# In the first turn of the experts, the second run of gathers moves behind the last gate tile, and the gate products wait for their own chunk only

## The chip, the cores and the metric

The kernel runs on one core of a Trainium2 chip. The metric is the device time of one execution in microseconds (us); the runs shown are three executions of the same program. Five engines work side by side and meet at semaphores: TensorE (PE, with its weight loads shown apart as PEld), VectorE (DVE), ScalarE (ACT), GpSimd (POOL) and SyncE (SP), which here issues the loads of the weights.

## The reference, cut to what matters

Two blocks are computed on 256 tokens of width 1024. The second one has two layers, and each ends in a mixture of 32 experts of width 256, of which every token uses two:

```
act = jax.nn.silu(jnp.einsum("td,edh->teh", t, w_g[sl])) * jnp.einsum("td,edh->teh", t, w_u[sl])
out = out + jnp.einsum("teh,ehd->td", act * combine[:, sl, None], w_d[sl])
```

`t` are the modulated tokens, `combine` holds the router's weights (zero but for the two chosen experts), and `sl` picks the experts of one group. This mixture, run once in each of two layers, is the only place that the change touches.

## The kernel before

The experts are taken in pairs: `PAIRS` is 16, and a **turn** `p` works on pair `p`. An expert has 64 places (`SLOTS`) for its tokens, so a pair fills 128. Token rows are picked by products with 0/1 matrices (`select`), which is called a gather; the tokens lie in a high and a low part (`hhi`, `hlo`), and both are multiplied. One gather serves four experts (two turns) for one chunk `c` of 128 of the 1024 features, and is four matmuls into PSUM. ACT or DVE then scales, shifts and writes it to `xg`. The weights come in tiles of 512 KB, twelve for each pair: eight (`gu`, k = 0 to 7, one for each chunk of features, gate and up side by side) and four (`d`). SP loads them in their order of use into a ring of 16 places (`RING`), and loads a place again when the semaphore `pe_tile` says that PE has used the tile that lay there.

`moe_events` writes the order of the work once, and PE, ACT and DVE each walk it, doing only their part of an event. The events are:

- `first` c: the gather of chunk c for turns 0 and 1, into PSUM bank c % 4. Even chunks are written to `xg` by ACT (semaphore `g_high`), odd ones by DVE (`g_copy`).
- `rest` j: DVE writes more columns of `select` (`slots_ready`).
- `gu` p, k: two products of `xg` with weight tile k for each of the two experts, into bank 0. The first of a turn waits for `mprod`, since it writes over bank 0.
- `V` p: PE turns `select` round into bank 1, ACT copies it (`selectT_ready`), DVE sums two numbers from it (`wslot_read`).
- `G` p, k: two gathers for a later pair of turns into bank 1, the first and second run of a turn (k = 0, 1). ACT writes both to `xg` (`g_high`). The second run waits until the first has been read.
- `A` p: ACT takes silu of the gate half of bank 0, and DVE multiplies it with the up half (`mprod`).
- `T` p: PE transposes that product; `d`: the down products; `Y` and `S`: scale the result and scatter it to the tokens.

On PE, `gu` (0, 0) waits in `gather_read` for all eight chunks of `first`, and the other seven products of turn 0 then wait for their weight tile alone. The events of turn 0, which has no `T`, `d`, `Y` or `S`, run: `gu` 0, `gu` 1, `gu` 2, `gu` 3, `V`, `gu` 4, `G` 0, `gu` 5, `gu` 6, `G` 1, `gu` 7, `A`. Turn 1 begins with `gu` 0, `gu` 1, `T` 0. The semaphore waits that matter are these:

```python
# gather_read
eng.wait_ge(s("g_high"), G_ACT_ALL * l + DC // 2 + 2 * p)
eng.wait_ge(s("g_copy"), G_DVE_ALL * (l + 1))
# ACT, event A
act.wait_ge(s("pe_tile"), moe_tile(l, "gu", p, 7) + 1)
act.activation(pair_a[:, 0, :], work[0][:, 0:T], ACT.Silu).then_inc(s("msilu"), 1)
```

In the rows below L1415 is a matmul of a gather, L1461 one of `gu`, L1435 one of `V`, L1474 one of `T`, L1486 one of `d`. On ACT, L1914 writes `xg`, L1922 is `V`, L1931 is the silu of `A`. On DVE, L2661 is `rest`, L2717 writes `xg`, L2728 is `V`, L2732 is the product of `A`.

Of the kernel before, what the change touches and what calls it, by code (L numbers as in the profile page):

```python
# [113 lines left out]
def moe_events(event):  # L114


    def turn(p):
        d, scatter, gather = p >= 1, p >= 2, p // 2 + 1 < FOURS
        event("gu", p, 0)
        if p == 0:  # L120
            event("rest", 0, 1)
        event("gu", p, 1)
        if d:
            event("T", p - 1, 0)
        event("gu", p, 2)
        if p == 0:
            event("rest", 0, 2)
        event("gu", p, 3)
        event("V", p, 0)
        if scatter:  # L130
            for j in range(3):
                event("S", p - 2, j)
        event("gu", p, 4)
        if d:
            event("d", p - 1, 0)
            event("d", p - 1, 1)
        if gather:
            event("G", p, 0)
        event("gu", p, 5)
        event("gu", p, 6)  # L140
        if d:
            event("d", p - 1, 2)
        if gather:
            event("G", p, 1)
        event("gu", p, 7)
        event("A", p, 0)
        if d:
            event("d", p - 1, 3)
            event("Y", p - 1, 0)
            event("Y", p - 1, 1)  # L150
    for c in range(DC):
        event("first", 0, c)
    event("rest", 0, 0)
    for p in range(PAIRS):
        turn(p)
    event("T", PAIRS - 1, 0)
    event("d", PAIRS - 1, 0)
    event("d", PAIRS - 1, 1)
    event("S", PAIRS - 2, 0)
    event("S", PAIRS - 2, 1)  # L160
    event("Y", PAIRS - 1, 0)
    event("S", PAIRS - 2, 2)
    event("d", PAIRS - 1, 2)
    event("d", PAIRS - 1, 3)
    event("Y", PAIRS - 1, 1)
    for j in range(3):
        event("S", PAIRS - 1, j)
# [3 lines left out]
G_ACT_ALL, G_DVE_ALL = DC // 2 + 2 * (PAIRS - 2), DC // 2  # L171
# [83 lines left out]
def moe_tile(l, what, p, k):  # L255
    return START[f"moe{l}"] + moe_place(what, p, k)
# [200 lines left out]
def program(nc, wstream, ada_d, c_d, consts_d, params_d, x_d, mem_d, rows_d, out_d):  # L457
    with ExitStack() as ctx:
        sems = {}

        def s(name):
            name = SHARED.get(name, (name, 0))[0]
            if name not in sems:
                sems[name] = ctx.enter_context(nc.semaphore(name))
            return sems[name]
# [146 lines left out]
        def gather_read(eng, l, p):  # L612

            eng.wait_ge(s("g_high"), G_ACT_ALL * l + DC // 2 + 2 * p)
            eng.wait_ge(s("g_copy"), G_DVE_ALL * (l + 1))
# [132 lines left out]
        def _(pe):  # L748
# [63 lines left out]
            def tile_ready(r, i=None, turn=6):  # L812
                if r in NUMBER:
                    pe.wait_ge(s("lo_done"), along(NUMBER[r] + 1, i, turn))
                    return whi[NUMBER[r] % AHEAD], wlo[NUMBER[r] % AHEAD]
                tile_loaded(pe, r, i, turn)
                return tiles[SLOT[r]], None
# [303 lines left out]
            def event(what, n, part=None):  # L1121
# [169 lines left out]
                elif what == "cmp_values":  # L1291
                    pe.wait_ge(s("pct_ready"), 1)
                    for j in range(HPG):
                        for g in range(GROUPS):
                            mm = pe.matmul(work[2 + j // 2][DH * g:DH * g + DH, (j % 2) * T:(j % 2) * T + T],
                                           vcmp[:, g, j, :], pcT[:, g, :],
                                           start=False, stop=False, skip_group_check=True)
                    mm.then_inc(s("cmp_values"), 1)
            mixer_events(event)

            pe.wait_ge(s("olo_ready"), 6)
# [14 lines left out]
            for l in range(LAYERS):  # L1316
                k = 7 + 3 * l
# [94 lines left out]
                def gather(bank, c, sel, at=0):  # L1412
                    for j, tok in enumerate((tok_hi, tok_lo)):
                        for q in range(QT):
                            mm = pe.matmul(work[bank][:, at:at + T], tok[:, q * D + c * P:q * D + (c + 1) * P],  # L1415
                                           sel(q), start=(j + q == 0), stop=(j + q == 2), skip_group_check=True)
                    return mm

                def event(what, p, k):
# [21 lines left out]
                    elif what == "G":  # L1441
                        if k == 0:
                            pe.wait_ge(s("selectT_ready"), base + p + 1)
                            pe.wait_ge(s("wslot_read"), 2 * (base + p + 1))
                        else:
                            pe.wait_ge(s("g_high"), G_ACT_ALL * l + DC // 2 + 2 * p + 1)
                        n = 2 * (p // 2 + 1)
                        for j in range(2):
                            mm = gather(1, 4 * (p % 2) + 2 * k + j,
                                        lambda q: select[:, q, n:n + 2, :].rearrange("p n t -> p (n t)"), j * T)  # L1450
                        mm.then_inc(s("g_mm"), 1)
                    elif what == "gu":
                        if k == 0 and p % 2 == 0:
                            gather_read(pe, l, p)
                        if k == 0:
                            pe.wait_ge(s("mprod"), base + p)
                        r = moe_tile(l, "gu", p, k)
                        w, _ = tile_ready(r)
                        for e in range(2):
                            a = (2 * (p % 2) + e) * SLOTS  # L1460
                            mm = pe.matmul(work[0][SLOTS * e:SLOTS * e + SLOTS, :], xg[:, p // 2 % 2, k, a:a + SLOTS],  # L1461
                                           w[:, e * 512:(e + 1) * 512], start=(k == 0), stop=(k == DC - 1),
                                           skip_group_check=True)
                        mm.then_inc(s("pe_tile"), 1)
                    elif what == "T":
                        pe.wait_ge(s("mprod"), base + p + 1)
                        pe.wait_ge(s("act_turned"), base + p)
                        if p < PAIRS - 2:
                            pe.wait_ge(s("g_high"), G_ACT_ALL * l + DC // 2 + 2 * (p + 1))
                        else:  # L1470
                            pe.wait_ge(s("selectT_ready"), base + p + 1)
                            pe.wait_ge(s("wslot_read"), 2 * (base + p + 1))
                        for f in range(2):
                            mm = pe.transpose(work[1][:, T + f * P:T + (f + 1) * P], pair_b[:, 0, f * P:(f + 1) * P], ident)  # L1474
                        mm.then_inc(s("turn_mm"), 1)
                    elif what == "d":
                        if k == 0:
                            pe.wait_ge(s("act_turned"), base + p + 1)
                        if p >= 1 and k % 2 == 0:
                            pe.wait_ge(s("y_low"), 2 * (base + p) - 1 + k // 2)  # L1480
                        r = moe_tile(l, "d", p, k)
                        w, _ = tile_ready(r)
                        half, f = k // 2, k % 2
                        for e in range(2):
                            own = slice(SLOTS * e, SLOTS * e + SLOTS)
                            mm = pe.matmul(work[2 + half][own, :], turned[:, f, own], w[:, e * 512:(e + 1) * 512],  # L1486
                                           start=(f == 0), stop=(f == 1), skip_group_check=True)
                        mm.then_inc(s("pe_tile"), 1)
                    elif what == "S":
                        if k == 0:  # L1490
                            pe.wait_ge(s("y_low"), 2 * (base + p) + (1 if p == PAIRS - 1 else 2))
                        sel = selectT[:, p, :]
                        for m in range(*S_PART[k]):
                            if p == PAIRS - 1 and m == DC // 2:
                                pe.wait_ge(s("y_low"), 2 * (base + p) + 2)
                            for y in (yshi, yslo):
                                mm = pe.matmul(acc_c[:, m, :], y[:, m * P:(m + 1) * P], sel, start=False,  # L1497
                                               stop=False, skip_group_check=True)
                            if (p, m) in S_LAST:
                                mm.then_inc(s("s_last"), 1)  # L1500
                        if k == 2:
                            mm.then_inc(s("s_mm"), 1)
                moe_events(event)
            norm_sum(7 + 3 * LAYERS)
            norm_row(7 + 3 * LAYERS, 0)
# [1423 lines left out]
```

## Time and profile before

| | |
|---|---|
| median of 3 runs | 1733.84 us (1732.2 to 1735.55) |
| the profiled execution's own time | 1735.7 us |
| its span in the trace | 1734.0 us |
| PE busy | 1660.4 us, 96% of the span |
| DVE, ACT busy | 936.6 us (54%), 647.7 us (37%) |
| chain that ended last | PE 75%, DVE 15%, ACT 7% |

An execution's own time is 1.7 us above its span. A busy share is the time in which an engine had an instruction at work; the chain is followed back from the last instruction, at each step to what released it. The two runs of the experts lie at 1011 to 1280 us and at 1451 to 1720 us from the span's start.

### The profile page before, as it was taken

Reading aid. Unit: us, or ns where it says so; the run is one execution under the profiler, and the core shown is the slowest. Engines: PE = TensorE matmul, PEld = TensorE weight load, DVE = VectorE, ACT = ScalarE, POOL = GpSimd, SP = SyncE. Lnnn points to the kernel's source line nnn. Section 1 sums busy time; section 2 is a strip of 40 time slices with the busy share of each in tenths; the row PEclk is TensorE's granted clock in tenths of the full one; section 3 lists DMA queues with packets and bytes.
Section 4 is the critical chain, followed back from the end, with each engine's and each line's share of the span. In section 5 each row is a group of like instructions: output and inputs, shape, how many; then the busy total and the mean of one; then the engine's idle time right before and its main releaser. Section 6 shows DMA issues by size and latency. Waiting matters only on the chain.

```text
span 1734.0 us, 29081 instructions
## 1 busy us (share of the span) xinstructions
PE 1660.4 (96%) x11261; PEld 1331.7 (77%) x11271; DVE 936.6 (54%) x1654; ACT 647.7 (37%) x1060; POOL 3.7 (0%) x9
## 2 busy tenths in 40 slices
PE   9999999999989999999999989999999998999998
PEld 8999989899878989999898954444469895444444
DVE  6888878753454768888697641111149864111112
ACT  5543456223355543333513332222243243222222
POOL 0000000000000000000000000000000000000000
PEclk9999999898799999999899999999999999999998
DMA  8998835113333549888243659999944355999993
GB/s 309 364 364 306 282 133 182 60 39 103 129 109 123 169 155 349 306 304 289 102 147 112 250 201 389 376 391 378 385 174 146 113 203 220 379 388 380 382 386 133
DMA packets 115806, 420.96 MB, mean 243 GB/s; under 512 B 12944, under 2 KB 13088, under 8 KB 115568
## 3 DMA queue, kind: packets, MB, share of 16 engines
q1 hardware_dynamic: 114624, 414.19, 65.3%
q0 software_dynamic: 1072, 5.21, 0.8%
q8 instruction: 80, 1.31, 0.3%
q14 instruction: 30, 0.25, 0.1%
HBM read 416.73 MB, written 2.62 MB: 242 GB/s over the span
## 4 chain that ended last, share of the span: by engine, by line
PE 75%; DVE 15%; ACT 7%; issue 3%; DVEq 0%; ACTq 0%
PE work L825 19%; PE work L1461 12%; PE acc L825 11%; DVE yconv L2496 6%; PE work L1486 5%; PE work L917 5%; PE work L1415 4%; PE acc L1497 3%; PE work L785 2%; ACT whi L1521 2%; ACT xg L1914 2%; PE work L860 2%; DVE wlo L1968 2%; PE work L902 1%; PE work L795 1%
## 5 line engine op out<-in xcount | busy, mean ns | idle before, releaser
L1968 DVE TENSOR_TENSOR wlo<-raw,whi 128x1024 fp32r<-128x1024 f32 x264 | 321.5, 1224 | 190.7 <-ACT whi L1521 190.2
L1521 ACT ACTIVATE whi<-raw 128x1024 fp32r<-128x1024 f32 x264 | 277.1, 1056 | 284.7 <-PE work L825 188.0
L825 PE MATMUL work<-hhi,whi 128*128 128x256 f32 x1024 | 293.2, 286 | 1.7 <-DVE hlo L1996 0.8
L825 PE MATMUL work<-hlo,whi 128*128 128x256 f32 x1024 | 291.6, 285 | 0.0
L825 PE MATMUL work<-hhi,wlo 128*128 128x256 f32 x1024 | 291.4, 285 | 0.0
L825 PEld LDWEIGHTS work<-hhi,whi 128*128 128x128 f32 x1024 | 198.2, 194 | 3.8 <-DVE wlo L1968 2.5
L825 PEld LDWEIGHTS work<-hlo,whi 128*128 128x128 f32 x1024 | 198.3, 194 | 0.1
L825 PEld LDWEIGHTS work<-hhi,wlo 128*128 128x128 f32 x1024 | 198.3, 194 | 0.0
L2732 DVE TENSOR_TENSOR pair_b<-work,pair_a 128x256 f32<-128x256 f32 x32 | 13.6, 425 | 309.5 <-ACT pair_a L1931 309.5
L1914 ACT ACTIVATE xg<-work,mod,gscale 128x256 f32<-128x256 f32 x120 | 61.7, 561 | 224.6 <-PE work L1415 224.6
L1461 PE MATMUL work<-over_splits,xg 128*64 128x512 f32 x480 | 120.8, 607 | 6.7 <-DVE pair_b L2732 6.2
L2074 DVE SCALAR_TENSOR_TENSOR ada_tiles<-ada_tiles,c_act 128x1024 f32<-128x1024 f32 x96 | 116.3, 1219 | 1.7 <-DMA ada_tiles<-ada_d 1.7
L860 PE MATMUL work<-hf,raw 128*128 128x256 f32 x512 | 113.3, 383 | 0.0
L860 PEld LDWEIGHTS work<-hf,raw 128*128 128x128 f32 x512 | 98.8, 193 | 13.9
L1461 PE MATMUL work<-raw,xg 128*64 128x512 f32 x408 | 101.7, 606 | 4.3 <-DVE pair_b L2732 2.3
L825 PE MATMUL acc<-ahi,whi 128*128 128x256 f32 x352 | 99.5, 283 | 2.9 <-DVE alo L2109 2.9
L917 PE MATMUL work<-hhi,whi 128*128 128x256 f32 x288 | 86.8, 302 | 15.2 <-ACT gates L1529 10.7
L2496 DVE SCALAR_TENSOR_TENSOR yconv<-vpad,params,yconv 128x256 f32<-128x256 f32 x240 | 99.4, 479 | 1.4
L825 PE MATMUL acc<-alo,whi 128*128 128x256 f32 x352 | 98.9, 281 | 0.0
L825 PE MATMUL acc<-ahi,wlo 128*128 128x256 f32 x352 | 98.7, 281 | 0.0
L917 PE MATMUL work<-hlo,whi 128*128 128x256 f32 x288 | 84.9, 295 | 0.0
L917 PE MATMUL work<-hhi,wlo 128*128 128x256 f32 x288 | 83.8, 291 | 0.0
(426 smaller groups left out, 2985.9 us busy)
## 6 DMA issues: line engine op xcount, KB each, us to landing
raw<-wstream_d SPq DMA_DIRECT2D x448, 512.0 KB, 4.7
over_splits<-wstream_d SPq DMA_DIRECT2D x192, 512.0 KB, 5.9
ada_tiles<-ada_d SPq DMA_DIRECT2D x96, 512.0 KB, 5.2
over_pool<-wstream_d SPq DMA_DIRECT2D x48, 512.0 KB, 6.2
bias_rows_d<-rt POOLq DMA_DIRECT2D x1, 1536.0 KB, 11.4
xT<-x_d SPq DMA_DIRECT2D x4, 256.0 KB, 4.2
mem_in<-mem_d POOLq DMA_DIRECT2D x1, 1024.0 KB, 5.3
tb<-bias_rows_d POOLq DMA_DIRECT2D x1, 1024.0 KB, 7.3
```

The lines of the kernel that those rows point to most:

```text
L825: mm = pe.matmul(out, a, b, start=(start and k == 0), stop=(stop and k == n - 1), skip_group_check=skip)
L860: mm = pe.matmul(work[bank][:, 0:T], h[:, c * P:(c + 1) * P], hf[:, c, :], start=(c == 0), stop=(c == DC - 1))
L917: mm = pe.matmul(bank[:, 0:T], ((h, h, l)[k % 3])[:, c * P:(c + 1) * P], ((hhi, hlo, hhi)[k % 3])[:, c, :], start=(k == 0), stop=(k == 23))
L1415: mm = pe.matmul(work[bank][:, at:at + T], tok[:, q * D + c * P:q * D + (c + 1) * P], sel(q), start=(j + q == 0), stop=(j + q == 2), skip_ ...
L1461: mm = pe.matmul(work[0][SLOTS * e:SLOTS * e + SLOTS, :], xg[:, p // 2 % 2, k, a:a + SLOTS], w[:, e * 512:(e + 1) * 512], start=(k == 0), ...
L1486: mm = pe.matmul(work[2 + half][own, :], turned[:, f, own], w[:, e * 512:(e + 1) * 512], start=(f == 0), stop=(f == 1), skip_group_check=True)
L1497: mm = pe.matmul(acc_c[:, m, :], y[:, m * P:(m + 1) * P], sel, start=False, stop=False, skip_group_check=True)
L1521: act.activation(whi[n % AHEAD][:], tiles[SLOT[SPLITS[n]]][:], ACT.Copy).then_inc(s("hi_done"), 1)
L1914: return act.activation(out, src, ACT.Identity, bias=mod[:, b:b + 1], scale=gscale[:, g:g + 1])
L1968: dve.tensor_tensor(wlo[n % AHEAD][:], tiles[SLOT[SPLITS[n]]][:], whi[n % AHEAD][:].bitcast(F32), ALU.subtract).then_inc(s("lo_done"), 1)
L2074: dve.scalar_tensor_tensor(ada_tiles[:, k, :], ada_tiles[:, k, :], 1.0, c_act[:], ALU.mult, ALU.mult, accum_out=out).then_inc(s("ada_done" ...
L2496: ins = dve.scalar_tensor_tensor(yconv[:, c, :], vpad[:, c, i:i + T], w, yconv[:, c, :], ALU.mult, ALU.add)
```

## The change

Three things, all for turn 0 of the experts alone, in both layers. The event `G` 0, 1 stands behind `gu` 7 and `A`, and no longer between `gu` 6 and `gu` 7. The first gate product on PE waits for the first three chunks that ACT writes (chunks 0, 2 and 4; bank 0, into which it writes, held chunks 0 and 4). Each later gate product of turn 0 waits for its own chunk, on `g_high` or `g_copy`, beside its weight tile.

```diff
@@ moe_events, turn(p)
         event("gu", p, 6)
         if d:
             event("d", p - 1, 2)
-        if gather:
+        if gather and p > 0:
             event("G", p, 1)
         event("gu", p, 7)
         event("A", p, 0)
+        if gather and p == 0:
+            event("G", p, 1)
         if d:
             event("d", p - 1, 3)
             event("Y", p - 1, 0)
@@ PE, event gu
                     elif what == "gu":
-                        if k == 0 and p % 2 == 0:
+                        if p == 0 and k % 2 == 0:
+                            pe.wait_ge(s("g_high"), G_ACT_ALL * l + max(k // 2 + 1, 3))
+                        elif p == 0:
+                            pe.wait_ge(s("g_copy"), G_DVE_ALL * l + k // 2 + 1)
+                        elif k == 0 and p % 2 == 0:
                             gather_read(pe, l, p)
                         if k == 0:
                             pe.wait_ge(s("mprod"), base + p)
```

On PE, the first products of turn 0 behind the gathers of `first` (`work<-select` is a gather, `work<-raw,xg` a gate product; the names in brackets are the semaphores waited for, `loaded` with a number being the weight tile's place). Before:

```order
L1415 MATMUL work<-select,hlo 128x256 x2
L1461 MATMUL work<-raw,xg 64x512 [waits mprod,loaded5,g_copy,g_high]
L1461 MATMUL work<-raw,xg 64x512
L1461 MATMUL work<-raw,xg 64x512 [waits loaded0]
L1461 MATMUL work<-raw,xg 64x512
L1461 MATMUL work<-raw,xg 64x512 [waits loaded1]
```

After:

```order
L1417 MATMUL work<-select,hlo 128x256 x2
L1467 MATMUL work<-raw,xg 64x512 [waits loaded5,mprod,g_high]
L1467 MATMUL work<-raw,xg 64x512
L1467 MATMUL work<-raw,xg 64x512 [waits loaded0,g_copy]
L1467 MATMUL work<-raw,xg 64x512
L1467 MATMUL work<-raw,xg 64x512 [waits loaded1,g_high]
```

The instructions are the same; the first product has lost its wait for `g_copy` and asks a lower count of `g_high`, and each later tile has gained one wait.

On PE, the end of turn 0 and the first product of turn 1 (`over_pool` and `over_splits` are weight tiles as `raw` is). Before:

```order
L1461 MATMUL work<-over_pool,xg 64x512 [waits loaded6]
L1461 MATMUL work<-over_pool,xg 64x512
L1415 MATMUL work<-select,hhi 128x256 [waits g_high]
L1415 MATMUL work<-select,hhi 128x256
L1415 MATMUL work<-select,hlo 128x256 x2
L1415 MATMUL work<-select,hhi 128x256 x2
L1415 MATMUL work<-select,hlo 128x256 x2
L1461 MATMUL work<-over_pool,xg 64x512 [waits loaded7]
L1461 MATMUL work<-over_pool,xg 64x512
L1461 MATMUL work<-over_splits,xg 64x512 [waits loaded11,mprod]
```

After:

```order
L1467 MATMUL work<-over_pool,xg 64x512 [waits loaded6,g_high]
L1467 MATMUL work<-over_pool,xg 64x512
L1467 MATMUL work<-over_pool,xg 64x512 [waits loaded7,g_copy]
L1467 MATMUL work<-over_pool,xg 64x512
L1417 MATMUL work<-select,hhi 128x256 [waits g_high]
L1417 MATMUL work<-select,hhi 128x256
L1417 MATMUL work<-select,hlo 128x256 x2
L1417 MATMUL work<-select,hhi 128x256 x2
L1417 MATMUL work<-select,hlo 128x256 x2
L1467 MATMUL work<-over_splits,xg 64x512 [waits loaded11,mprod]
```

The second run of gathers now lies between the last gate product of turn 0 and the product of turn 1 that waits for `mprod`.

On ACT, the same place, from the first run's write of `xg` to the copy of `T` 0 (L1934, L1940 after). Before:

```order
L1914 ACTIVATE xg<-work,mod,gscale 128x256 [waits g_mm]
L1914 ACTIVATE xg<-work,mod,gscale 128x256
L1914 ACTIVATE xg<-work,mod,gscale 128x256 [waits g_mm]
L1914 ACTIVATE xg<-work,mod,gscale 128x256
L1931 ACT_TABLE_LOAD
L1931 ACTIVATE pair_a<-work 128x256 [waits pe_tile]
L1934 ACTIVATE pair_a<-work 128x256 [waits turn_mm]
```

After:

```order
L1920 ACTIVATE xg<-work,mod,gscale 128x256 [waits g_mm]
L1920 ACTIVATE xg<-work,mod,gscale 128x256
L1937 ACT_TABLE_LOAD
L1937 ACTIVATE pair_a<-work 128x256 [waits pe_tile]
L1920 ACTIVATE xg<-work,mod,gscale 128x256 [waits g_mm]
L1920 ACTIVATE xg<-work,mod,gscale 128x256
L1940 ACTIVATE pair_a<-work 128x256 [waits turn_mm]
```

The load of silu's table and the silu have moved ahead of the write of the second run, and no further table load has come in. DVE and SP have the instructions that they had, in the same order.

## Rows read from the trace of the kernel before

**Rows 1.** The page, busy time of each engine over the span.
```profile
PE 1660.4 (96%) x11261; PEld 1331.7 (77%) x11271; DVE 936.6 (54%) x1654; ACT 647.7 (37%) x1060; POOL 3.7 (0%) x9
```

**Rows 2.** Windows in the experts: us, each engine's busy time, PEclk, DMA share, GB/s.
```profile
1017.00:1037.00 20.00, 17.58 (x86) 7.14 (x86) 5.26 (x12) 4.86 (x9) 0.00 (x0) 1.00 0.79 283
...
1217.00:1237.00 20.00, 19.92 (x108) 9.30 (x106) 2.15 (x5) 5.22 (x11) 0.00 (x0) 1.00 1.00 383
```

**Rows 3.** Timeline, layer 0, turn 0 begins: start us, us, engine, line, work [idle].
```profile
1014.42 0.40 PE L1415 MATMUL work<-select,hhi 128*128 128x256 f32 x2
...
1015.09 0.56 ACT L1914 ACTIVATE xg<-work,mod,gscale 128x256 f32<-128x256 f32 x1 [0.53 <-PE work L1415]
...
1015.57 0.54 DVE L2717 TENSOR_SCALAR xg<-work,gscale,mod 128x256 f32<-128x256 f32 x1 [0.40 <-PE work L1415]
...
1016.07 0.40 PE L1415 MATMUL work<-select,hlo 128*128 128x256 f32 x2
1016.51 0.54 DVE L2717 TENSOR_SCALAR xg<-work,gscale,mod 128x256 f32<-128x256 f32 x1 [0.40 <-PE work L1415]
...
1017.16 3.65 PE L1461 MATMUL work<-raw,xg 128*64 128x512 f32 x16 [0.68 <-ACT xg L1914]
```

**Rows 4.** Timeline, layer 0, the end of turn 0.
```profile
1023.59 1.02 ACT L1914 ACTIVATE xg<-work,mod,gscale 128x256 f32<-128x256 f32 x2 [1.82 <-PE work L1415]
...
1024.39 1.03 PE L1461 MATMUL work<-over_pool,xg 128*64 128x512 f32 x4
...
1025.35 0.50 PE L1415 MATMUL work<-select,hhi 128*128 128x256 f32 x2
...
1026.16 0.40 PE L1415 MATMUL work<-select,hlo 128*128 128x256 f32 x2
...
1026.48 1.08 PE L1461 MATMUL work<-over_pool,xg 128*64 128x512 f32 x4
1026.59 1.02 ACT L1914 ACTIVATE xg<-work,mod,gscale 128x256 f32<-128x256 f32 x2 [1.98 <-PE work L1415]
1027.63 1.28 ACT L1931 ACT_TABLE_LOAD   x1
1028.92 0.38 ACT L1931 ACTIVATE pair_a<-work 128x256 f32<-128x256 f32 x1
1029.34 0.42 DVE L2732 TENSOR_TENSOR pair_b<-work,pair_a 128x256 f32<-128x256 f32 x1 [7.12 <-ACT pair_a L1931]
...
1029.82 1.94 PE L1461 MATMUL work<-over_splits,xg 128*64 128x512 f32 x8 [2.26 <-DVE pair_b L2732]
```

**Rows 5.** Timeline of PE, layer 1, the same two places.
```profile
1457.15 3.65 PE L1461 MATMUL work<-raw,xg 128*64 128x512 f32 x16 [0.68 <-ACT xg L1914]
...
1469.81 1.94 PE L1461 MATMUL work<-over_splits,xg 128*64 128x512 f32 x8 [2.26 <-DVE pair_b L2732]
```

**Rows 6.** Timeline, layer 0, `rest` and `V` of turn 0, and the first run.
```profile
1016.97 4.23 DVE L2661 TENSOR_TENSOR select<-consts,rt 128x256 fp32r<-128x256 f32 x6
...
1020.74 0.44 PE L1435 MATMUL work<-identr,select 128*128 128x128 f32 x2
...
1021.38 0.39 ACT L1922 ACTIVATE selectT<-work 128x256 fp32r<-128x256 f32 x1 [4.79 <-PE work L1438]
1021.87 0.35 DVE L2728 TENSOR_REDUCE rt<-work 64x1 f32<-64x2 f32 x2 [0.67 <-ACT selectT L1922]
...
1022.36 0.48 PE L1415 MATMUL work<-select,hhi 128*128 128x256 f32 x2
```

**Rows 7.** Timeline of ACT, layer 0, its table load ahead of the first gather's write.
```profile
1010.66 1.28 ACT L1914 ACT_TABLE_LOAD   x1 [4.88 <-DVE overflow L2658]
...
1012.29 0.56 ACT L1914 ACTIVATE xg<-work,mod,gscale 128x256 f32<-128x256 f32 x1 [0.34 <-PE work L1415]
```

**Rows 8.** Waits of SP's DMA queue, 1000 to 1270 us: total us, times, longest.
```profile
SPq L654 <- PE work L1461: 141.2, 118, 20.6
```

**Rows 9.** DMA issues of 1200 to 1240 us: count, KB each, median us to landing.
```profile
over_splits<-wstream_d SPq DMA_DIRECT2D x16, 512.0 KB, 6.6
```

## The prediction

> **What bounds the kernel now.** I read the busy shares first: PE is at work 96% of the span [rows 1]. A change can then win where PE stands still, or by taking work from it, and this one takes no work. So I looked at the windows through the experts. In the steady part PE is busy 19.92 of 20 us, but in the first window of a layer's experts only 17.58 [rows 2]: some 2.4 us are idle there, and that is the stretch that the diff edits. The timeline of that stretch shows where they are. The reader is to look for the brackets on PE's rows. Of idle time above 0.1 us that a wait explains there are two pieces, 0.68 us ahead of the first gate product of turn 0 [rows 3] and 2.26 us ahead of the first gate product of turn 1 [rows 4]. In layer 1 the same two rows carry the same 0.68 and 2.26 [rows 5]. Every later engine in the experts works from what PE gives it, and PE's own stream hardly pauses after this, so what is won here should reach the end.
>
> **The first wait: chunks instead of all of them.** Before, the first gate product waits for the last copy, which is DVE's of chunk 7: it starts at 1016.51 and takes 0.54, so it ends at 1017.05, and the product starts at 1017.16 [rows 3]. (The row names ACT as the releaser; ACT's write of chunk 6 was done before, DVE's end fits the start.) After, it needs the third write of ACT, 1015.09 + 0.56 = 1015.65 [rows 3]. That is earlier than PE itself is ready. PE's last pair of gather matmuls starts at 1016.07 [rows 3], and the distance from such a last pair to a gate product with nothing to wait for is 1026.48 - 1026.16 = 0.32 us [rows 4]. The product would start at 1016.39, **0.77 us earlier**. The later ones have slack: chunk 5 is there at 1015.57 + 0.54 = 1016.11, chunk 7 at 1017.05 [rows 3], and five gate products, at about 0.86 us each, run before chunk 5 is asked for.
>
> The added waits, one for each of seven tiles, I cost at nothing. The nearest rows are the gathers of chunks 4 to 7, each of which waits for `g_high` or `g_copy` too: the pairs of matmuls from 1014.42 to 1016.07 are seven steps, 0.236 us a step, without a break at the chunk's border [rows 3]. The bound from the other side is the 0.68 us that PE stood still when such a wait was really late; it is priced below, as a rival.
>
> **What limits the shift at once.** `V` moves from 1020.74 to 1019.97, ACT's copy from 1021.38 to 1020.61 (0.39 long, done at 1021.00), and DVE's two sums could start at 1021.87 - 0.77 = 1021.10. But DVE is then in the six selections of `rest`, which hang on its copy of chunk 7 and don't move: 1016.97 + 4.23 = 1021.20 [rows 6]. The sums start 0.10 later than the shift would have them. The first run of gathers waits for them (it starts 0.49 behind their start), so it moves from 1022.36 to 1021.69: **0.67 us are left of the 0.77**. `V` itself needs the first two selections and chunk 7's copy; both are there long before 1019.97.
>
> **The second wait: the last gate tile ahead of the gathers.** Before, the order on PE is `gu` 6 at 1024.39, the second run at 1025.35, `gu` 7 at 1026.48, and then nothing until 1029.82 [rows 4]. In between lies a chain on two other engines: ACT writes the second run (1026.59, 1.02 us), loads silu's table (1.28), takes silu (0.38), DVE multiplies (0.42), and PE goes on. With the shift of 0.67, after the change:
>
> - `gu` 6 starts at 1023.72. A gate tile is four matmul records. Sixteen in a row take 3.65 us [rows 3] and four 1.08, so each further record adds 0.214, and `gu` 7 starts 0.86 later, 1024.58.
> - The second run follows a gate tile by 1025.35 - 1024.39 = 0.96, so at 1025.54, and what stands behind it follows by 1026.48 - 1025.35 = 1.13: the first gate product of turn 1 could start at **1026.67**, as far as PE goes.
> - ACT is free of the first run at 1023.59 + 1.02 - 0.67 = 1023.94. Its table load then ends by about 1025.24. `gu` 7 ends at 1024.58 + 1.03 = 1025.61, and silu can start at about 1025.64. From silu's start to PE's next gate product it is 1029.82 - 1028.92 = 0.90 [rows 4]: 1026.54.
>
> The later of the two is PE's own, by 0.13 us. The product of turn 1 moves from 1029.82 to 1026.67, **3.15 us earlier**, first gain included. What covers the ACT chain is the second run of gathers, 1.13 us of PE work that was on the path before and is on it still; were it shorter by over 0.13, the rest would be idle.
>
> That the table load is out of the way needs that ACT takes it before it waits for `gu` 7. In the order it stands ahead of the silu, and the wait is written on the silu. The earlier load shows that this holds: ACT begins it at 1010.66, and the activation behind it, which waits for the gather, at 1012.29, idle for 0.34 us after the load [rows 7].
>
> The Trainium skill (ScalarE: Activation LUTs, What ACT_TABLE_LOAD costs) states 1.28 us for the load and 1.38 us more for a drain, 2.66 us for each switch. This trace has the 1.28 but shows no drain: the write of `xg` ends at 1027.61 and silu starts at 1028.92. By the page's figure silu would start at 1026.60 after the change and turn 1 at 1027.50, an estimate from that page, and both layers together would give 4.6 us; I go by the row.
>
> **Who waits next.** ACT's write of the second run now stands behind silu. Its last pair starts at 1025.54 + 0.81 and ends 0.40 later, 1026.75; ACT is done with silu at 1026.02. The write ends near 1027.80. `T` 0 needs it and comes two gate products after 1026.67, near 1028.5: hidden by 0.7 us. SP gets the weight tiles' places earlier, below. Nothing else is moved past anything.
>
> **The sum.** 3.15 us in layer 0, and layer 1 has the same idle pieces [rows 5], so 6.3 us. Against the profiled execution's own 1735.7 us that is 1729.4; that execution lies 1.9 us above the median, so against the median, 1733.84 - 6.3 = **1727.5 us**, 0.36% faster. Nothing under 0.2% (3.5 us) can be told from no change here.
>
> **The rivals.**
>
> *The weights don't come faster.* The DMA engines' share in the steady part is 1.00, at 383 GB/s [rows 2]. If the stream of weights were what really paces the experts, PE would start each layer 3 us earlier and wait for tiles later, and the time would stay at **1733.8**. For it speaks that full share. Against it: over 1000 to 1270 us the queue of loads waited 141.2 us for PE to free a place, in 118 waits [rows 8]. At 383 GB/s a tile of 524,288 bytes takes 1.37 us, a turn of the ring of 16 places 21.9 us, and 6.6 us after its issue a tile is there [rows 9]. So it lies ready some 15 us before its use, five times what is won. Chance 0.10.
>
> The Trainium skill (HBM Reference, Specifications) puts a core's part of the memory's bandwidth at about 358 GB/s, and says that a core streaming alone gets more, about 425. The trace, at 383, is above the first figure; only the first would make this rival the likeliest.
>
> *The table load stays on the path*, because ACT takes it only when `gu` 7 is done. Silu then starts at 1025.64 + 1.30 = 1026.94, turn 1 at 1027.84; 1.98 us a layer, 4.0 in all: **1729.8**. Rows 4 alone allow it, since there the load begins just as both conditions are met; rows 7 speak against it. Chance 0.09.
>
> *The single waits cost more than the idle time they replace.* Each of turn 0's seven later tiles has two waits now. If PE could no longer bring the next tile's stationary operand in ahead of such a wait, each border would cost up to the 0.68 us of a late one. Seven are 4.8 us a layer against 3.15 won: 1.6 lost, twice, **1737.1**. It decides from 0.45 us a border. Against it stand the gathers of chunks 4 to 7, with their waits and no break [rows 3]. Chance 0.04.
>
> **How the numbers follow.** The forecast, 5 to 7 us won, gets 0.73; the rivals 0.10, 0.09 and 0.04; 0.04 is left for what I don't see. The range must cover the forecast, the table's rival at 1729.8 and the scatter of the median (some 1.7 us either way in the runs of before): 1725.0 to 1731.6. It leaves out the weights' rival and the slower one. Faster by over 0.2%, that is below 1730.4: nearly all of the forecast and some two thirds of the table's rival, 0.80. Within 0.2%: the weights' rival, a third of the table's and a little of the rest, 0.15. Slower: 0.05.
>
> **What the changed profile would show.** First product of turn 0 about 0.32 us after the last gather pair and no bracket of 0.68 on it; DVE's sums right at the end of the selections; ACT's table load starting at the end of the first run's write, over before `gu` 7 ends; the first product of turn 1 with no idle time above some 0.1 us, 10.3 us after the first of turn 0 where it was 12.7; the first window with PE busy above 19; and SP's waits for PE still there through the experts, with tiles landing in 5 to 7 us. It is wrong if PE shows waits for DMA later in the experts, if the table load begins only behind `gu` 7, or if turn 0's tiles stand further apart than 0.86 us.

## The result

Four runs of the changed kernel have a median of 1722.69 us (1721.74 to 1724.3), against 1733.16 us of before; the ratio is 0.9932, 95% interval 0.9916 to 0.9948. It is 10.5 us faster, where 6.3 were forecast; the time lies 2.3 us below the range. Timed again (run 2 below) the ratio is 0.9942 (0.9928 to 0.9956), 10.0 us. So both the forecast's mechanism and something that it left out have to be found in the traces. Two disturbed executions of run 17 (1850.79 and 8536.54 us) stand in no mean below.

### The edited stretch, after

Timeline of the changed kernel in layer 0, the rows that answer to [rows 3, 4 and 6] (start us, us, engine, line, work, idle before it):

```profile
1012.87 0.39 PE L1417 MATMUL work<-select,hlo 128*128 128x256 f32 x2
1013.19 3.65 PE L1467 MATMUL work<-raw,xg 128*64 128x512 f32 x16
...
1013.76 4.22 DVE L2667 TENSOR_TENSOR select<-consts,rt 128x256 fp32r<-128x256 f32 x6
...
1017.91 0.34 DVE L2734 TENSOR_REDUCE rt<-work 64x1 f32<-64x2 f32 x2
...
1019.62 1.02 ACT L1920 ACTIVATE xg<-work,mod,gscale 128x256 f32<-128x256 f32 x2 [1.82 <-PE work L1417]
1020.42 1.89 PE L1467 MATMUL work<-over_pool,xg 128*64 128x512 f32 x8
1020.66 1.28 ACT L1937 ACT_TABLE_LOAD   x1
...
1022.24 0.51 PE L1417 MATMUL work<-select,hhi 128*128 128x256 f32 x2
1022.36 0.39 ACT L1937 ACTIVATE pair_a<-work 128x256 f32<-128x256 f32 x1 [0.41 <-PE work L1467]
...
1022.77 0.42 DVE L2738 TENSOR_TENSOR pair_b<-work,pair_a 128x256 f32<-128x256 f32 x1 [4.52 <-ACT pair_a L1937]
...
1023.38 1.94 PE L1467 MATMUL work<-over_splits,xg 128*64 128x512 f32 x8
1023.49 1.02 ACT L1920 ACTIVATE xg<-work,mod,gscale 128x256 f32<-128x256 f32 x2 [0.75 <-PE work L1417]
```

Both brackets of idle time are gone from PE. The first gate product stands 0.32 us behind the last pair of gathers (1.09 before), and the first product of turn 1 comes 10.19 us behind that of turn 0 (12.66 before; 10.28 forecast). Together 0.77 + 2.47 = 3.24 us a layer. The table load runs while PE is still in the last two gate tiles, ACT then waits 0.41 us for the last of them, and its write of the second run follows silu without holding anybody. In layer 1 PE's two first products stand at 1449.92 and 1460.10, 10.18 apart.

The windows that answer to [rows 2] (us, each engine's busy time, PEclk, DMA share, GB/s) show PE at work all through the first 20 us. The transfers' share rose in the first window, 0.86 for 0.79, and is 0.99 for 1.00 in the steady part:

```profile
1013.00:1033.00 20.00, 20.00 (x103) 8.59 (x103) 5.66 (x12) 6.27 (x12) 0.00 (x0) 1.00 0.86 319
1213.00:1233.00 20.00, 19.91 (x106) 9.14 (x105) 2.15 (x5) 5.38 (x11) 0.00 (x0) 1.00 0.99 377
```

SP's waits for gate products over 1000 to 1270 us are 138.7 us in 116 waits, where [rows 8] had 141.2 in 118. PE's own waits over 1018 to 1275 us are 2.1 us for the product of silu, 0.5 for ACT and 0.4 for DVE, and none for a weight tile.

### The rest of the difference

The spans are 1734.0 and 1722.0 us, 12.0 apart, and the edits account for 2 x 3.24 = 6.5. The remainder lies where the two programs are the same, at the start and at the end. The first weight products, and the 32 small matmuls of the last norm's sum, before:

```profile
16.23 0.55 PE L825 MATMUL work<-hhi,whi 128*128 128x256 f32 x1 [0.82 <-DVE hlo L1996]
16.58 0.42 PE L825 MATMUL work<-hlo,whi 128*128 128x256 f32 x1
...
1719.73 6.04 PE L785 MATMUL work<-ones,hf 128*128 128x1 f32 x32 [0.33 <-ACT hf L1534]
```

The same in the changed kernel:

```profile
14.56 0.35 PE L827 MATMUL work<-hhi,whi 128*128 128x256 f32 x1 [0.82 <-DVE hlo L2002]
14.75 0.28 PE L827 MATMUL work<-hlo,whi 128*128 128x256 f32 x1
...
1710.00 3.70 PE L787 MATMUL work<-ones,hf 128*128 128x1 f32 x32 [0.33 <-ACT hf L1540]
```

The reader is to compare the duration of like matmuls: 0.42 against 0.28 us, and 6.04 against 3.70 for the same 32 at the end. That is the clock's lower and upper level (1.2 and 2.4 GHz). The windows say so for the end, where the granted clock is 0.56 over 1720 to 1726 us before and 1.00 over 1710 to 1714 after. For the start the durations alone speak, since the window of 15 to 20 us has 1.00 in both; but in run 16 the same products took 0.55 and 0.44 us, and the granted clock of that window is 0.50 there. The changed kernel is 3.2 us ahead when it comes to the first gather of layer 0 (1007.82 against 1011.03), and wins 2.3 us more in the last sum. Whether that is chance or comes with the edit is what most of the experiments are about.

### The profile page after: what moved, and what is told of

Read it like the earlier page. It is cut to its first block, busy times and chain, and to the rows that moved or that the text cites. A ratio compares the mean times of both kernels' runs of the same rounds, so it can differ in the third digit from the quotient of the medians.

```text
span 1722.0 us, 29103 instructions
## 1 busy us (share of the span) xinstructions
PE 1653.5 (96%) x11271; PEld 1323.7 (77%) x11271; DVE 935.8 (54%) x1654; ACT 647.5 (38%) x1060; POOL 3.7 (0%) x9
## 4 chain that ended last, share of the span: by engine, by line
PE 75%; DVE 15%; ACT 6%; issue 3%; DMA 0%; SPq 0%; DVEq 0%; ACTq 0%
PE work L827 19%; PE work L1467 13%; PE acc L827 11%; DVE yconv L2502 6%; PE work L1492 5%; PE work L919 5%; PE work L1417 4%; PE acc L1503 3%; PE work L787 2%; ACT whi L1527 2%; DVE wlo L1974 2%; PE work L862 2%; ACT xg L1920 2%; PE work L904 1%; PE work L797 1%
```

## The experiments

"Mean" is that of all timed runs; the profile is of one of them. Ratios are to the kernel before on the same chip. "Theory A" and its fellows are the readings that the expectations set against each other.

**Run 1, before again.** No edit.

> The kernel of before, unchanged, timed against itself. In the profiles the edited stretches gave 3.4 us in layer 0 and 3.4 us in layer 1, which is 6.7 of the 12.0 us between the two spans; 3.2 us more came in the first 65 us of the program and 2.2 us in its last 10 us, where TensorE's granted clock stood at its lower level in the one and at its upper level in the other. Theory A, the two further pieces come from where the clock happens to stand in an execution: this copy scatters by 2 to 4 us from run to run, a ratio of 1.000 with an interval of 0.15% or more, and its profile may show another clock at the start or the end than before's. Theory B, they belong to the program: the copy repeats before's start (first products at 16.2 us, half clock) and end (32 products of the last sum in 6.0 us).

Ratio 1.000 (0.9989 to 1.001), mean 1735.15 of 12. The trace repeats before's start (16.13 us) and even each mark up to 1719 us within 0.4 us, but its last sum took 3.70 us, not 6.04. So the start belongs to the program as profiled (for theory B), and the end doesn't (for theory A).

**Run 2, the changed kernel again.** No edit.

> The changed kernel as it is, timed again beside before on one chip. Theory A (the clock at the start and the end is chance): on average over ten runs a gain nearer to 6.5 us than to 10.5, with single runs from 1722 to 1731. Theory B (a property of the program): again 10.5 us, 1722 to 1724, and again a full clock at 14.6 us and in the last sum (3.7 us).

Ratio 0.9942, mean 1725.62 of 6, 1723.84 to 1726.75: 10 us again, tightly. The trace has the upper clock at the start (first weight product at 14.62) and in the last sum (3.70). "Nearer to 6.5" is refuted.

**Run 3, the waits alone**

```diff
-                        if k == 0 and p % 2 == 0:
+                        if p == 0 and k % 2 == 0:
+                            pe.wait_ge(s("g_high"), G_ACT_ALL * l + max(k // 2 + 1, 3))
+                        elif p == 0:
+                            pe.wait_ge(s("g_copy"), G_DVE_ALL * l + k // 2 + 1)
+                        elif k == 0 and p % 2 == 0:
```

> Only the waits of the gate products of turn 0 are changed; the second run of gathers stays ahead of the last gate tile. Between the first gather and the first product of turn 1 it should win 0.67 us in each layer (0.77 less what the selections on DVE hold back), 1.3 us in all: that step of the prediction. Theory A: total 1.3 us give or take 2. Theory B: if the further 4 to 5 us hang on the program being changed at all, 5 to 6 us.

Ratio 0.9985 (0.9973 to 0.9997), mean 1734.09. In layer 0 it is 18.06 us from the first gather to turn 1, where before has 18.79: 0.73, a little above the expected 0.67. In layer 1 it is 19.35 us against 18.91, because the gathers ran at the lower clock (granted 0.50 over 1447 to 1453 us); from turn 0's first product to turn 1's it is 12.66 as in every trace of the old order. The trace shows a second thing there, in the product behind the idle 2.26 us:

```profile
1027.80 1.94 PE L1465 MATMUL work<-over_splits,xg 128*64 128x512 f32 x8 [2.26 <-DVE pair_b L2736]
...
1466.55 3.33 PE L1465 MATMUL work<-over_splits,xg 128*64 128x512 f32 x8 [2.26 <-DVE pair_b L2736]
```

The same eight matmuls behind the same idle time took 1.94 us in layer 0 and 3.33 in layer 1. Over 1466 to 1472 us the granted clock is 0.72. PE stood still for 2.26 us and its clock fell. From turn 1's start to DVE's first write of `xT` behind the experts it then took 249.84 us, where layer 0 of the same trace took 248.25: the fall cost 1.6 us.

**Run 4, the move alone**

```diff
-        if gather:
+        if gather and p > 0:
             event("G", p, 1)
         event("gu", p, 7)
         event("A", p, 0)
+        if gather and p == 0:
+            event("G", p, 1)
```

> Only the second run of gathers is moved behind the last gate tile; the first product still waits for all eight chunks. Between the first gather and the first product of turn 1 it should win 2.4 to 2.5 us in each layer, 4.9 us in all. Rival of the prediction (silu's table load stays on the path): 1.2 us a layer. Theory A: total 4.9 us give or take 2. Theory B: 9 us.

Ratio 0.9964 (0.9953 to 0.9976), mean 1729.93, 6 us. The stretch takes 16.57 and 16.44 us: 2.2 and 2.5 won. The table load's rival is out, the first wait of 0.68 us is there as before. The parts, 2 and 6 us, make some 8, not 10; but each is known to 2 us only, so this doesn't yet show that more than the sum is there. Behind the experts of layer 0 this trace lost 1.9 us to before's, though it has no idle time ahead of turn 1: more on this below.

**Run 5, before with a longer start and a held end.** `hold` issues matmuls on zeros.

```diff
-            hold(1, 8)
-            norm_sum(0)
+            hold(1, 24)
+            norm_sum(0, (0, 2, 2, 2))
...
-            norm_row(0, 0)
+            norm_row(0, 12)
...
-            norm_sum(7 + 3 * LAYERS)
+            norm_sum(7 + 3 * LAYERS, (2, 2, 2, 2))
```

> The kernel before with more matmuls on zeros that nobody reads: 24 for 8 at the start, two ahead of each part of the first norm's sum, 12 behind its row, and two ahead of each part of the last norm's sum. They are to bring TensorE's clock up before the first weight products and hold it up in the last sum. Theory A, the further 3 to 4 us of the changed kernel come from the clock at the start: this one starts its weight products at the upper level (pairs 0.12 us apart, not 0.21) and reaches the first gather of layer 0 some 3 us nearer to the changed kernel's time; in all 2 to 4 us faster than before, unless the 16 more matmuls delay the first sum by up to 2 us. Theory B, the further gain has its cause in the experts: no change against before, or slower by the added matmuls.

Ratio 0.9993 (0.9984 to 1.0002), mean 1734.02. The weight products started at 21.43 us for 16.23, and the first gather came at 1010.73 for 1011.03: what the clock gave, the longer start took, and the expected 2 to 4 us did not come.

**Run 6, the changed kernel with the same.**

> The changed kernel with the same added matmuls on zeros. Theory A: with the same clock at start and end in both, the difference to the kernel before with these matmuls is that of the edited stretches, 6.3 to 6.8 us, and not 10. Theory B: it stays 10 us.

Ratio 0.9946 (0.9927 to 0.9965), mean 1726.07. The pair's means differ by 8.0 us, between the two expectations; the two traces differ by 6.9, with the first gather at 1010.73 and 1010.34.

**Run 7, silu behind the second run on ScalarE**, TensorE as changed.

```diff
-        event("A", p, 0)
         if gather and p == 0:
             event("G", p, 1)
+        event("A", p, 0)
```

> The changed kernel, but ScalarE (and with it VectorE) takes silu of turn 0 behind its write of the second run of gathers, as before the change; TensorE's program is that of the changed kernel, instruction for instruction. The write ends at 1024.51 in the changed kernel's trace, the table load takes 1.28 and from silu's start to the next product it is 0.90: turn 1 should start near 1026.7 instead of 1023.4, 3.3 us lost a layer, 6.6 in all, about 1732. If the cover by the second run of gathers were not what matters, it would lose less than 2. Theory A (start and end by chance of the clock) or a start that goes with TensorE's program: its first products start at the upper clock as the changed kernel's do (14.6 us) if the start goes with TensorE's program, at either level if it is chance.

Ratio 1.0001 (0.9985 to 1.0016), mean 1735.10: the whole gain is gone. PE's rows:

```profile
1027.93 2.37 PE L1467 MATMUL work<-over_splits,xg 128*64 128x512 f32 x8 [3.27 <-DVE pair_b L2738]
...
1030.85 2.84 PE L1467 MATMUL work<-over_splits,xg 128*64 128x512 f32 x8
```

The idle time is 3.27 us, as worked out (3.3), and what stands behind it ran at the lower clock (2.84 for the usual 1.94; granted 0.77 over 1026 to 1032 us). In layer 1 the same 3.27 us left the clock up. Against the changed kernel's trace 6.66 us are lost in the two edited stretches, 1.7 by this fall and 1.85 in the code behind the experts of layer 0. PE's program is that of the changed kernel, but the first weight product took 0.55 us (at 14.30), the lower level: the start doesn't go with PE's program.

**Run 8, the new order in every turn**

```diff
-        if gather and p > 0:
-            event("G", p, 1)
         event("gu", p, 7)
         event("A", p, 0)
-        if gather and p == 0:
+        if gather:
             event("G", p, 1)
```

> The changed kernel, with the second run of gathers behind the last gate tile and silu in every turn that gathers, not in turn 0 alone. In the changed kernel's trace TensorE still waits 2.1 us a layer for the product of silu, in 7 turns, 0.3 us each, since ScalarE writes the second run (1.02 us) ahead of silu. With silu first that wait should go: 2 us a layer, 4 us in all, against the changed kernel. Rival: the transposes of the next turn wait for the later write of the run; they come two gate products behind, 1.9 us, and the write ends 1.4 us after the run, so nothing is lost there.

Ratio 0.9897 (0.9875 to 0.9918), median 1718.55, mean 1718.07: the fastest kernel of the study, 7.5 us below the changed kernel's mean. The waits for the product of silu have left the list; this is all that 1015 to 1265 us has:

```profile
PE work L1490 <- ACT pair_a L1938: 0.5, 1, 0.5
```

From turn 1's first product to DVE's first write of `xT` it took 245.1 us in layer 0 and 245.0 in layer 1, the changed kernel 248.3 and 248.2: 3.2 us a layer, where 2 were expected. Only 2.1 us of it are the waits that the list had; where the rest comes from stays open. Its start was at the lower clock (16.21 us) as before's was.

**Run 9, the idle time filled**, in the kernel before.

```diff
+                        if (p, k) == (1, 0):
+                            for _ in range(7):
+                                pe.matmul(work[2][:, :], zero[:, :], spread(zero[:, 0:1], (512,), (0,)),
+                                          start=True, stop=True)
```

> The kernel before, with seven matmuls on zeros (0.21 us each, 1.5 in all) into a bank that is free then, between the last gate product of turn 0 and the first of turn 1, where TensorE stands idle for 2.26 us. The path is untouched: profiled span and edited stretches as before (12.66 us from turn 0's first product to turn 1's). Theory C: in a part of the executions the clock falls behind that idle time, as in the waits-only kernel's layer 1, where the eight products behind it took 3.33 us and not 1.94; closing the idle time saves that too. Then this kernel's mean lies 1 to 2 us under before's and its slow runs (1738 to 1741) are rarer. Without theory C: mean the same within 0.5 us.

Ratio 0.9998 (0.999 to 1.0007), mean 1734.63 against 1734.84 of the 23 executions of before beside it. The path is untouched (12.66 us), the idle time 0.63. None of its 11 executions was above 1735.7; of before's 23 executions six were, from 1736.3 to 1741.6. Four of these six have a mean granted clock of 0.960, and none of the 11 is below 0.962. That fits theory C without showing it, and the mean moved by 0.2 us, not 1 to 2.

**Runs 10, 11, 13 to 16, other starts.** `hold(1, 8)` becomes `hold(1, 12)`, `(1, 10)` and `(1, 16)`, in the kernel before and in the changed one.

> The kernel before with 12 matmuls on zeros at the start for 8, so that TensorE is at work for longer before the first norm's sum. Theory A: its clock rises within these, the 32 products of the first sum take some 3.7 us and not 7.0, its weight products start at the upper level, and it is 2 to 3 us faster than before. Rival: the four more only delay the sum by 1 to 2 us and the clock rises no sooner.

> The changed kernel with the same 12 matmuls at the start. Its start was at the upper clock for the first sum already, so it should gain nothing or lose up to 1 us. Theory A: against the kernel before with 12, 6.4 us from the edited stretches and what theory C adds, 7 to 8 us, not 10.

> The kernel before with 10 matmuls on zeros at the start for 8: only the place of the clock's changes against the program is shifted. Theory A: mean within 2 us of before's, edited stretches 37.7 us as in every trace of this order. Theory D: the same; the pair decides.

> The changed kernel with 10 for 8. Edited stretches 31.3 to 31.5 us. Theory A: the difference of this pair's means differs from the 10 us by 2 or more and is between 5 and 9. Theory D: 9 to 10 us again.

> The kernel before with 16 for 8: the start shifts further. Same reading as with 10; 0 to 3 us slower for the longer wait of the first sum.

> The changed kernel with 16 for 8. Theory A: a third value for the pair's difference, with the mean over all pairs near 7. Theory D: 9 to 10 us once more.

The ratios of before's order are 0.9999, 1.0006 and 0.9994 (12, 10, 16), those of the changed order 0.9947, 0.9939 and 0.9941. The start alone is worth nothing that can be told, though with 12 and 16 the first gather came 1.8 and 2.0 us earlier than in the trace of before, and the gain is 9 to 12 us in each pair: theory A, as far as it means the start, isn't borne out. (In runs 10 and 11 the first weight product took 0.55 us, so the rise of the clock by then, which run 10 was to bring, didn't come.) The traces show other differences. In the pair with 16 the first gather comes at 1009.05 and 1008.97 us, so the start is level, and still the spans differ by 8.9: 6.4 in the edited stretches and 2.3 behind turn 1 of layer 1, which is the last sum. And in two of the three traces of before's order the clock fell behind the 2.26 us. Run 10:

```profile
1028.35 2.66 PE L1461 MATMUL work<-over_splits,xg 128*64 128x512 f32 x8 [2.26 <-DVE pair_b L2732]
```

Run 13:

```profile
1027.56 2.52 PE L1461 MATMUL work<-over_splits,xg 128*64 128x512 f32 x8 [2.26 <-DVE pair_b L2732]
```

**Run 12, all turns with 12 at the start and the end held**

> A version that may beat all: the second run of gathers and silu in the new order in every turn, 12 matmuls on zeros at the start, and two ahead of each part of the last norm's sum. All turns alone gave 1718.1 us on average with a start at the lower clock; the start should add 2 us, the end 1 us where the clock falls in the last sum: 1715 to 1716. Rival: the start brings nothing, 1717 to 1718.

Ratio 0.9916 (0.9904 to 0.9929), mean 1719.40. 1715 to 1716 were expected. Its profiled execution is the fastest of those profiled (1716.53), but the mean isn't under run 8's: the added matmuls bring nothing that can be told.

**Runs 17 and 18, level.** Both with 16 at the start and the last sum held as in run 5; the kernel before also with run 9's filling.

> The kernel before with 16 matmuls on zeros at the start, seven in the idle time ahead of turn 1, and two ahead of each part of the last norm's sum: the clock is held up in both places where traces of the old order lose it. Theory E (the surplus is the clock at these two places): 1.9 us from the end and 1 us from the idle time, 1731 to 1732 on average, against 1734.1 with the 16 alone. If they are not the cause: 1734.

> The changed kernel with the same 16 at the start and the same matmuls in the last sum (it has no idle time ahead of turn 1 to fill). Theory E: the end costs it 0.5 us, 1725.1, and the difference to the levelled kernel before is the 6.4 us of the edited stretches, 6 to 7. Otherwise the difference stays at 9 to 10.

The means are 1732.9 of ten and 1726.0 of six, 6.9 us apart. By the ratios, 0.9990 (0.9977 to 1.0003) and 0.9944 (0.9925 to 0.9962), it is 8 us. Run 17 was expected at 1731 to 1732: it missed that, and its ratio can't be told from 1. The two traces are only 3.8 us apart, because the start now goes the other way (first gather at 1007.63 and 1010.48). So this pair fits theory E without proving it.

## Why the prediction was wrong

What each trace says, from the starts on PE's timeline and the span ("between" is from turn 1 of layer 0 to the first gather of layer 1, "rest" from turn 1 of layer 1 to the end):

| trace | first gather | gather to turn 1, layers 0, 1 | between | rest |
|---|---|---|---|---|
| before | 1011.03 | 18.79, 18.91 | 421.08 | 264.2 |
| run 1, before again | 1011.02 | 18.82, 18.92 | 421.21 | 261.9 |
| run 9, filled | 1010.57 | 18.83, 18.91 | 421.13 | 264.1 |
| run 10, before, 12 | 1009.20 | 19.15, 18.90 | 424.37 | 261.8 |
| run 13, before, 10 | 1008.53 | 19.03, 18.93 | 424.39 | 264.2 |
| run 15, before, 16 | 1009.05 | 18.90, 18.92 | 421.24 | 264.2 |
| run 3, waits alone | 1009.74 | 18.06, 19.35 | 419.40 | 265.4 |
| run 4, move alone | 1010.30 | 16.57, 16.44 | 423.15 | 261.8 |
| run 7, silu behind | 1009.03 | 18.90, 19.01 | 424.54 | 261.8 |
| changed | 1007.82 | 15.56, 15.69 | 421.03 | 261.9 |
| run 2, changed again | 1007.89 | 15.82, 15.65 | 420.98 | 261.9 |
| run 11, changed, 12 | 1007.15 | 15.74, 15.67 | 420.97 | 261.9 |
| run 14, changed, 10 | 1007.98 | 15.58, 15.67 | 421.10 | 261.9 |
| run 16, changed, 16 | 1008.97 | 15.69, 15.69 | 421.18 | 261.9 |

**The mechanism was right, in both halves.** 3.0 to 3.5 us a layer in the pairs of traces without a held end, 3.25 on average, where 3.15 were worked out. The first wait gave 0.77. The 0.10 us that the selections on DVE were to hold back were not there: DVE's sums started 4.72 us behind the first gate product, as before (4.71), and overlapped the end of the selections by 0.07. That is why turn 1 came at 10.19 and not 10.28. Silu's chain was covered by the second run of gathers as drawn; run 7 took that cover away and lost it all. The added waits cost nothing (turn 0's first 16 gate products took 3.65 us as before), and the three rivals are out: no table load on the path, no wait for weights. One reading was loose, without effect on the sum: the 2.4 us that [rows 2] have idle are nearly all the 2.26, since the 0.68 lie ahead of that window but for their last 0.16.

**The step that failed is the sum**, "against the median, 1733.84 - 6.3": it took for granted that all code outside the edited stretches keeps its time, and let only the scatter of a median widen the range, which it took from the 3.4 us between three executions. Later executions of before lie between 1730.3 and 1741.6 us. The code outside has a clock that changes with when it runs. In the two traces compared first it gave 3.2 us at the start and 2.3 in the last sum, 5.5 of the 12.0. Over all traces four places show:

- *The last norm's sum.* Its 32 matmuls took 5.6 to 6.1 us in five of the seven traces with before's order on PE and an unheld end (before, runs 3, 9, 13 and 15) and 3.70 in the other two (1 and 10). In all five of the changed kernel they took 3.70, and in runs 4, 7 and 8 too. 2.3 us hang on it.
- *The clock behind the idle 2.26 us.* It fell in 3 of the 14 places that the traces of kernels with this idle time offer (runs 3, 10 and 13), once in two behind run 7's 3.27 us, and never at this place in the traces without such idle time. From turn 1 to DVE's first write of `xT` a layer took 248.2 to 248.3 us without a fall, whatever the order of turn 0 (runs 8 and 12 apart, which change the later turns), and 249.8 to 250.0 with one: a fall cost 1.6 to 1.8 us. With that frequency it is some 0.7 us an execution, over both layers, as an estimate. The prediction priced this idle time at its own length; the trace that it read from happened to be one in which the clock held.
- *The start.* The first gather comes 3.1, 2.1, 0.6, 0.1, 0.4 and -2.9 us earlier in the changed member of the six pairs (runs 1 and 2, 10 and 11, 13 and 14, 15 and 16, 5 and 6, 17 and 18); over the kernels with different starts the timed mean moved by nothing that can be told.
- *The norm's sum behind the experts of layer 0.* "Between" is 424.4 in runs 10 and 13 for 421.2, and only half of the 3.2 us more is the fall. The other half is in this sum, the same kind of matmuls with one column, here in before and in run 10:

```profile
1281.36 4.72 PE L785 MATMUL work<-ones,hf 128*128 128x1 f32 x32 [1.57 <-ACT hf L1534]
...
1281.66 6.63 PE L785 MATMUL work<-ones,hf 128*128 128x1 f32 x32 [1.58 <-ACT hf L1534]
```

The granted clock over 1279 to 1292 us is 0.74 and 0.62. Run 4 has this too (5.92 us, "between" 423.15), without idle time or a fall ahead of it, so it can't be charged to the idle time. Run 3 is 1.7 us shorter between (419.40), which no edit of its explains either.

That the surplus is the clock, in the timed executions and not only in one trace of each, can be read from their mean granted clocks. An execution's time, times one less its granted clock, is an estimate, from above, of what the lower level cost it. Averaged over each run's executions it is smaller in the changed member of all six pairs, by 4.2, 3.0, 3.7, 2.8, 3.2 and 1.4 us (pairs in the order above, the levelled one last), 3.0 on average. What is left of the differences between the means (9.5, 9.7, 11.9, 9.4, 8.0 and 6.9 us) is 6.2 on average, against 6.4 from the edited stretches. The standard error is 0.4 to 2.1 us for one pair's figure of the clock and some 0.6 for the average.

Which place gives how much stays open. From the traces 1.6 us would come from the end (2.3 in five of seven) and 0.7 from the clock behind the idle time, 8.7 with the edits' 6.4. Run 9, which filled the idle time, moved its mean by 0.2 to 0.5 us, and runs 5 and 17 can't be told from before (0.9993 and 0.9990, intervals to 1.0002 and 1.0003). No run shows why five traces of the changed kernel agree at the end and seven of the old order don't.

The Trainium skill (TensorE: Matmul & The Clock Gate, What's actually happening) says that the clock's window runs freely and doesn't reset when a kernel starts. The repeated traces fit that only in part: in two executions of one program (before and run 1, changed and run 2) the marks kept within some 0.5 us up to the last sum. The timed executions do scatter: the 12 of run 1 have mean granted clocks from 0.961 to 0.967, at 1733.1 to 1738.5 us.

## What to carry to other kernels

Put the engine that everyone waits for a piece of work ahead of a wait on two other engines, and move the writes that nobody needs yet behind the chain that somebody does; where it helps in one turn, try it in all of them (here 10 us became 17). Idle time on TensorE of a few us can have a second price beside its length, the clock behind it (here 1.6 to 1.8 us, in 4 of 16 places), and one trace need not show it: look at the same place in several, and at the mean granted clock of every timed execution. And a change of 0.4% in one place can go with 3 us more or less in code that wasn't edited; leave room for it in the range, and before looking for a cause compare two traces mark by mark, code that is the same included.

## What the runs showed of the hardware

- Behind an idle time of 2.26 us TensorE's clock fell in 3 of 14 places, behind one of 3.27 us in 1 of 2, behind one of 0.63 us in none of 4. The eight matmuls behind it then took 2.4 to 3.3 us for 1.94, and the layer 1.6 to 1.8 us more.
- 32 matmuls with one column, one after the other, were done with a clock that fell during them in five of seven traces of the old order (5.6 to 6.1 us for 3.70, at the end of the program) and in none of the eight others with the same code there.
- The mean granted clocks of the timed executions of one program differ: 0.960 to 0.967 for before, with times of 1730.3 to 1741.6 us.
- A table load that stands ahead of a waiting activation is taken at once, while the activation waits (1020.66 in the changed kernel, with silu at 1022.36). No time beyond its 1.28 us was seen.
